# Diagonal blocks of the masked key products: strided row sums on VectorE in place of small products on TensorE

## The chip, the cores and the metric

The kernel runs on one core of one Trainium2 chip. The metric is device time in microseconds (us): the median of several executions. Engines are called TensorE or PE (matrix products; PEld is its weight load), VectorE or DVE, ScalarE or ACT, GpSimd or POOL, and SyncE or SP, which here issues transfers (DMA). Each engine takes its own instructions in order and waits on counters (semaphores) that other engines raise.

## The reference

One encoder layer over two sequences of 512 tokens, 1024 wide: an input projection whose columns feed 8 neighbourhood attention heads and 4 gated DeltaNet heads, an output projection, a layer norm, and a gated MLP with a depthwise convolution. The change is in the DeltaNet heads, the chunked delta rule. Cut to what matters (two of these run, one per direction):

```python
def _gated_delta_chunked(q, k, v, beta, g):
    ...
    gc = jnp.cumsum(g, axis=-1)
    ...
    decay = jnp.exp(jnp.where(tril, gc[..., :, None] - gc[..., None, :], -jnp.inf))
    kb = k * beta[..., None]
    lower = jnp.where(strict, jnp.einsum('bhnid,bhnjd->bhnij', kb, k) * decay, 0.0)
    a = lower + jnp.eye(c, dtype=jnp.float32)
    rhs = jnp.concatenate([v * beta[..., None], kb * jnp.exp(gc)[..., None]], axis=-1)
    sol = lax.linalg.triangular_solve(a, rhs, left_side=True, lower=True, unit_diagonal=True)
    ...
```

`lower` is the masked, decayed matrix of key products. The kernel solves with it by inverting its 16 x 16 diagonal blocks and joining the inverses level by level.

## The kernel before, in words

All arithmetic is in float32; the big projections are done as three products of split operands (`w_hi`, `w_lo`, `x_hi`, `x_lo`), with weights split by POOL. Stages follow each other: neighbourhood attention (to about 240 us), four delta heads (`delta_head(h, ...)`, h = 0 to 3, about 97 us each, to about 630 us), output projection and norm, the MLP. The order on each engine is written out by hand in one function per engine; each engine has its own `delta_head`.

In a delta head a sequence s (0 or 1) has 4 chunks (CH) of 128 tokens, and both directions g share the key products. On VectorE, in this order: `log_decays` (L1655, once the decay rows have landed), key scales, the convolution of Q for s = 0 (`convolve`, L1589, four instructions for one sequence), `lower` (L1667, from the key products in PSUM into `m_t`), then for each s the **join** of both directions' parts (L1739, into `m_t`) and the **mask** (L1741), which keeps in `u_t` only the 16 x 16 blocks on the diagonal of each 128 x 128 chunk. Then the convolutions of Q for s = 1 and of V for s = 0, two MEMSETs, and `eliminate` (L1684 to L1699), which inverts 128 blocks at once, one per partition, and raises `inv_ready`. Then the convolution of V for s = 1, `scores` (L1674), `between` (L1719), `both_directions` (L1712 to L1715) on the inverses that have come back, `expand` (L1704), `decayed_q` (L1678), and the level loop with its subtractions (L1784, L1785) and selections (L1723, L1727).

Between mask and elimination the blocks have to get from "row of the chunk per partition" to "block per partition". PE multiplies each chunk of `u_t` with `fold` (a column of 16 x 16 identities): a product of 128 x 128 by 128 x 16, whose row m holds the 16 entries of column m in its diagonal block. These products (L816) go into PSUM bank 6, after the wait for `masked` and for the copies of K out of that bank (`k_tok_ready`). ACT copies the bank into `packed` (L1307) and raises `fold_copied`. SP's `exchange` waits for that, stores `packed` to `block_dram` (L476), waits for the store, and loads the blocks twice: into half of the partitions of `packed` (L480) and into the other half of `blk` (L482). Since the two directions need a block and its transpose, `eliminate` begins with a turning copy of one half (L1684, partitions 64 to 127). After the elimination SP stores the inverses and loads them back (L485, L492).

On PE the head runs: projection of Q for s = 1 and V for s = 0 (`project`, L614), the products L816, projection of V for s = 1, projections of the gate z (two, with the key-query products L832 between them), V's transposes (L842; those for s = 1 wait for `fold_copied`, since they use bank 6), a first piece of the next head's K projection (`fill`, L639), and the level loop: L868 for both s, a fill of 5, L882 and L885 for both s, a fill of 5. At level 0 L868 waits for `c_ready` and `r_selected`, which VectorE raises in `between` and `expand`. Products of small tiles in float32 stand in the trace as two records each.

After the loop over chunks and the last products (L938, L939) the next head follows; after the fourth, the output projection (L951).

Of the kernel before, what the change touches and what calls it, by code (L numbers as in the profile page):

```python
# [8 lines left out]
AX = mybir.AxisListType  # L9

P = 128
# [21 lines left out]
CH = L // P  # L34
# [51 lines left out]
def encoder_layer(nc, xT, x_tok, ln_row, w_gate, w_all, rpb, gdn_conv, gate_vec, a_log,  # L86
# [3 lines left out]
    with ctx:  # L90
# [187 lines left out]
        def sem(name):  # L278
            names.append(name)
            return ctx.enter_context(nc.semaphore(name))  # L280
# [23 lines left out]
        ktr_done, k_tok_ready, vtr_done, vg_tok_ready, kk_done, kq_done = (  # L304
            sem("ktr_done"), sem("k_tok_ready"), sem("vtr_done"), sem("vg_tok_ready"), sem("kk_done"),
            sem("kq_done"))
        o_copied, masked, folded, fold_copied, blocks_stored, blocks_landed, eliminated = (
            sem("o_copied"), sem("masked"), sem("folded"), sem("fold_copied"), sem("blocks_stored"),
            sem("blocks_landed"), sem("eliminated"))
        inv_ready, inv_stored, d_landed, u_landed = (  # L310
            sem("inv_ready"), sem("inv_stored"), sem("d_landed"), sem("u_landed"))
# [100 lines left out]
        def _(sp):  # L412
# [59 lines left out]
            def exchange(h, last_head):  # L472

                sp.wait_ge(fold_copied, h + 1)
                sp.dma_start(block_dram.rearrange("(i b) (r c) -> (b r) i c", b=P // IB, c=IB), packed[:, 0:INST // 2, :]  # L476
                             ).then_inc(blocks_stored, 16)
                sp.wait_ge(blocks_stored, 16 * h + 16)
                half = P // 2
                sp.dma_start(packed[half:P, INST:2 * INST, :].rearrange("p i c -> p (i c)"), block_dram  # L480
                             ).then_inc(blocks_landed, 16)
                sp.dma_start(blk[0:half, :], block_dram).then_inc(blocks_landed, 16)  # L482

                sp.wait_ge(inv_ready, h + 1)
                sp.dma_start(inverse_dram.rearrange("m k n -> k m n"), inv[:, :, :]).then_inc(inv_stored, 16)  # L485
                sp.wait_ge(inv_stored, 16 * h + 16)

                for m, landed in enumerate((d_landed, u_landed)):
                    for d in range(2):
                        i0 = d * (INST // 2)  # L490
                        rows = inverse_dram[m ^ d, :, :].rearrange("(i b) (r c) -> (b r) i c", b=P // IB, c=IB)
                        sp.dma_start(packed[:, m * INST + i0:m * INST + i0 + INST // 2, :],  # L492
                                     rows[:, i0:i0 + INST // 2, :]).then_inc(landed, 16)
                for n in range(6, 8):
                    load(raw(GDN0 + n), 4 * h + (GDN0 + n))
                if not last_head:

                    sp.wait_ge(osum_done, 2 * h + 2)
                    load_decays(h + 1)
                for n in range(8, 10):  # L500
                    load(raw(GDN0 + n), 4 * h + (GDN0 + n))
# [100 lines left out]
        def _(pe):  # L602
# [182 lines left out]
            def tile(ap, c):  # L785
                return ap[:, c * P:(c + 1) * P]

            def delta_head(h, last_head):
# [19 lines left out]
                pe.wait_ge(w_ready, c + 3)  # L808
                pe.wait_ge(conv_done, 6 * h + 3)
                project(0, slot(GDN0 + 2), 0)  # L810
                pe.wait_ge(k_tok_ready, 2 * h + 1)
                for s in range(SEQS):
                    pe.wait_ge(masked, 2 * h + (s + 1))
                    for cc in range(CH):
                        n = s * CH + cc
                        ins = mm(ps[6][:, n * IB:(n + 1) * IB], tile(u_t[:, s, :], cc), fold, start=True, stop=True)  # L816
                ins.then_inc(folded, 1)

                pe.wait_ge(m_ready, 4 * h + 4)
                project(v_bank(1), slot(GDN0 + 2), 1)  # L820
                pe.wait_ge(w_ready, c + 4)
# [13 lines left out]
                for s in range(SEQS):  # L835
                    pe.wait_ge(silu_done, 6 * h + (4 + s + 1))
                    if s == 0:
                        pe.wait_ge(k_tok_ready, 2 * h + 2)
                    else:
                        pe.wait_ge(fold_copied, h + 1)  # L840
                    for cc in range(CH):
                        ins = nc.tensor.transpose(tile(ps[7 - s], cc), tile(qkv[:, VX, s, :], cc), ident)  # L842
                    ins.then_inc(vtr_done, 1)
# [273 lines left out]
        def _(act_e):  # L1117
# [134 lines left out]
            def delta_head(h, last_head):  # L1252
# [48 lines left out]
                for g in range(GROUPS):  # L1301
# [1 line left out]
                centre(h, QX, 1)  # L1303
                silu(QX, 0)
                centre(h, VX, 0)
                act_e.wait_ge(folded, h + 1)
                nc.scalar.copy(packed[:, 0:INST // 2, :].rearrange("p i c -> p (i c)"), ps[6][:, 0:INST // 2 * IB]  # L1307
                               ).then_inc(fold_copied, 1)
                silu(QX, 1)
                silu(VX, 0)  # L1310
                centre(h, VX, 1)
# [179 lines left out]
        def _(dve):  # L1491
# [139 lines left out]
            def chunks(ap):  # L1631
                return ap.rearrange("p (c n) -> p c n", c=CH)
# [5 lines left out]
            def delta_head(h, last_head):  # L1638
# [41 lines left out]
                def eliminate():  # L1680

                    half = slice(P // 2, P)
                    step(nc.vector.tensor_copy(blk[half, :].rearrange("p (r c) -> p r c", c=IB),  # L1684
                                               packed[half, INST:2 * INST, :].rearrange("p c r -> p r c")))
                    lo = blk[:, :].rearrange("p (i j) -> p i j", i=IB)
# [49 lines left out]
                for s in range(SEQS):  # L1736
                    dve.wait_ge(m_ready, 4 * h + (2 * s + 2))

                    TT(m_t[:, 2 * s, :], m_t[:, 2 * s, :], m_t[:, 2 * s + 1, :], ALU.add).then_inc(joined_l, 1)  # L1739
                    dve.wait_ge(joined_l, 2 * h + (s + 1))  # L1740
                    TT(chunks(u_t[:, s, :]), chunks(m_t[:, 2 * s, :]), bcast(same_block), ALU.mult).then_inc(masked, 1)  # L1741
                convolve(h, QX, 1)
                convolve(h, VX, 0)
                step(nc.vector.memset(inv[:, 0, :], 0.0))
# [329 lines left out]
```

## Time and profile before

| what | us |
|---|---|
| median of 3 runs | 1456.69 |
| lowest and highest run | 1456.39, 1457.8 |
| the profiled execution's own time | 1456.55 |
| its span, first to last instruction | 1454.8 |
| busy in it: PE, DVE, ACT, POOL | 1395.0, 788.5, 442.1, 479.6 |
| mean granted TensorE clock (1 is 2.4 GHz) | 0.991 |

The profile describes one execution. A busy share is an average over stages with different limits; what a stage waits for is read from the chain and the waits in it. In a timeline, "0.69 DVE L1741 ..." behind 357.31 means that the instruction started at 357.31 us and took 0.69; a row with x8 merges eight neighbours. In square brackets stands the time that the engine was idle before, and who ended it. The starts of two neighbouring VectorE instructions can be closer than the duration of the first, because they overlap a little at their ends.

### The profile page before, as it was taken

The page shows a single profiled execution, that of the slowest core. Times are in us where ns is not written, and L with a number is a line of the kernel's source. Part 1 is how long each engine was busy: PE and PEld are TensorE (multiplying, and loading weights), DVE is VectorE, ACT ScalarE, POOL GpSimd, SP SyncE. Part 2 cuts the span into 40 slices and gives each one's busy share as a digit, 9 for nine tenths or more (in the row PEclk, how much of TensorE's full clock was granted, in tenths as well). Part 3 has the DMA queues.
Part 4 walks back from the last instruction along what each step waited for, and adds up shares of the span by engine and source line. Part 5 has one row for each costly group of instructions (what it writes and reads, how often), then busy time and mean ns, then how long its engine had stood idle before and what let it go on. Part 6 is the DMA issues. An engine that isn't in the chain of part 4 may idle for free.

```text
span 1454.8 us, 18723 instructions
## 1 busy us (share of the span) xinstructions
PE 1395.0 (96%) x6959; PEld 1146.2 (79%) x6959; DVE 788.5 (54%) x1346; ACT 442.1 (30%) x924; POOL 479.6 (33%) x219
## 2 busy tenths in 40 slices
PE   7999999989899898799999999999999999999998
PEld 5777777777787787788878888888888888888886
DVE  4344447968868869633744344344344354226657
ACT  4234346327245163240522222121121122122210
POOL 3322221212121022126544344343343344454460
PEclk9999999999999999899999999999999999999999
DMA  8100011201102112033221111111111115111112
GB/s 249 45 30 30 30 44 44 50 16 60 34 23 58 29 58 50 15 131 107 90 79 45 56 43 48 53 43 51 50 43 55 46 43 193 53 43 53 49 58 101
DMA packets 49511, 87.15 MB, mean 60 GB/s; under 512 B 24432, under 2 KB 27184, under 8 KB 49456
## 3 DMA queue, kind: packets, MB, share of 16 engines
q1 hardware_dynamic: 44704, 70.41, 15.0%
q10 hardware_dynamic: 4752, 15.99, 2.9%
q8 instruction: 36, 0.59, 0.2%
q14 instruction: 19, 0.16, 0.0%
HBM read 76.66 MB, written 9.73 MB: 59 GB/s over the span
## 4 chain that ended last, share of the span: by engine, by line
issue 37%; PE 32%; DVE 16%; POOL 10%; DMA 3%; ACT 1%; POOLq 1%; SPq 0%; DVEq 0%; ACTq 0%
PE banks L639 11%; POOL w_hi L524 8%; PE banks L951 6%; PE banks L1051 3%; DVE qkv L1589 2%; DMA d_n<-decay_dram 2%; PE banks L614 1%; PE banks L748 1%; DVE att L1655 1%; PE banks L773 1%; DVE m_t L1667 1%; DVE d_n L1785 1%; PE banks L761 1%; DVE inv L1696 1%; DVE outer L1693 1%
## 5 line engine op out<-in xcount | busy, mean ns | idle before, releaser
L524 POOL TENSOR_TENSOR w_hi<-w_raw,one 128x1024 fp32r<-128x1024 f32 (+1 forms) x99 | 187.4, 1893 | 900.0 <-PE banks L614 368.3
L614 PE MATMUL banks<-x_hi,w_hi 128*128 128x512 f32 (+1 forms) x912 | 358.9, 393 | 15.8 <-POOL w_lo L527 8.3
L614 PE MATMUL banks<-x_hi,w_lo 128*128 128x512 f32 (+1 forms) x912 | 355.7, 390 | 0.0
L614 PE MATMUL banks<-x_lo,w_hi 128*128 128x512 f32 (+1 forms) x912 | 355.6, 390 | 0.0
L1905 DVE SCALAR_TENSOR_TENSOR cv<-banks,fw,cv 128x511 f32<-128x511 f32 x176 | 132.0, 750 | 261.7 <-ACT cv L1425 253.9
L527 POOL TENSOR_TENSOR w_lo<-w_raw,w_hi 128x1024 fp32r<-128x1024 f32 (+1 forms) x99 | 251.4, 2540 | 7.7
L614 PEld LDWEIGHTS banks<-x_hi,w_hi 128*128 128x128 f32 (+1 forms) x912 | 170.6, 187 | 54.9 <-POOL w_lo L527 8.3
L614 PEld LDWEIGHTS banks<-x_hi,w_lo 128*128 128x128 f32 (+1 forms) x912 | 170.6, 187 | 37.3 <-issue 0.6
L614 PEld LDWEIGHTS banks<-x_lo,w_hi 128*128 128x128 f32 (+1 forms) x912 | 170.7, 187 | 36.4 <-issue 1.1
L1425 ACT ACTIVATE cv<-banks,fw_j 128x512 f32<-128x512 f32 x88 | 68.7, 780 | 337.2 <-PE banks L614 334.7
L1934 DVE TENSOR_TENSOR a_lo<-act,a_hi 128x1024 fp32r<-128x1024 f32 x39 | 65.1, 1675 | 96.5 <-ACT a_hi L1443 96.5
L1051 PE MATMUL banks<-w_hi,a_hi 128*128 128x512 f32 x288 | 112.0, 389 | 0.0
L1051 PE MATMUL banks<-w_hi,a_lo 128*128 128x512 f32 x288 | 112.0, 389 | 0.0
L1051 PE MATMUL banks<-w_lo,a_hi 128*128 128x512 f32 x288 | 112.0, 389 | 0.0
L639 PE MATMUL banks<-x_hi,w_hi 128*128 128x512 f32 x256 | 103.7, 405 | 0.0
L639 PE MATMUL banks<-x_hi,w_lo 128*128 128x512 f32 x256 | 103.2, 403 | 0.0
L639 PE MATMUL banks<-x_lo,w_hi 128*128 128x512 f32 x256 | 103.1, 403 | 0.0
L1443 ACT CAST a_hi<-act 128x1024 fp32r<-128x1024 f32 (+1 forms) x39 | 40.8, 1053 | 147.3 <-PE banks L1051 139.3
L1589 DVE SCALAR_TENSOR_TENSOR qkv<-banks,cw_all,qkv 128x510 f32<-128x510 f32 (+1 forms) x96 | 71.3, 749 | 11.5 <-ACT qkv L1187 7.8
L1915 DVE TENSOR_TENSOR act<-cv 128x512 f32 (+1 forms) x44 | 68.4, 1554 | 9.1 <-DVE cv L1905 8.9
L1562 DVE TENSOR_TENSOR s_sb<-banks,bm 128x512 f32<-128x512 f32 x32 | 22.1, 692 | 76.7 <-PE banks L748 76.7
L1051 PEld LDWEIGHTS banks<-w_hi,a_hi 128*128 128x128 f32 x288 | 54.1, 188 | 11.3
(206 smaller groups left out, 2000.1 us busy)
## 6 DMA issues: line engine op xcount, KB each, us to landing
w_raw<-w_all SPq DMA_DIRECT2D x102, 512.0 KB, 3.2
d_n<-decay_dram SPq DMA_DIRECT2D x8, 512.0 KB, 4.7
z_tok<-x_tok ACTq DMA_DIRECT2D x8, 512.0 KB, 6.0
x_dram<-z_tok ACTq DMA_DIRECT2D x8, 512.0 KB, 2.6
z<-x_dram ACTq DMA_DIRECT2D x8, 512.0 KB, 8.2
y<-z SPq DMA_DIRECT2D x7, 512.0 KB, 2.6
mix<-xT SPq DMA_DIRECT2D x12, 256.0 KB, 8.4
gb<-ln_row ACTq DMA_DIRECT2D x4, 512.0 KB, 8.3
```

The lines of the kernel that those rows point to most:

```text
L524: nc.gpsimd.tensor_tensor(w_hi[u][:, 0:n], w_raw[ru][:, 0:n], one[:, :].to_broadcast([P, n]), ALU.mult).then_inc(w_high, 1)
L527: nc.gpsimd.tensor_tensor(w_lo[u][:, 0:n], w_raw[ru][:, 0:n], w_hi[u][:, 0:n].bitcast(F32), ALU.subtract).then_inc(w_ready, 1)
L614: last = mm(ps[bank][0:cols, :], w[u][:, k * cols:(k + 1) * cols], seq(x[:, k, :], s), start=n == 0, stop=n == 3 * KT - 1)
L639: ins = mm(ps[s][:, :], w[u][:, k * P:(k + 1) * P], seq(x[:, k, :], s), start=i == 0, stop=i == 3 * KT - 1)
L951: ins = mm(ps[b][:, :], x[k][:, t * P:(t + 1) * P], w[u][:, cols], start=k == 0 and n == 0, stop=k == KT - 1 and n == 2)
L1051: ins = mm(ps[t][:, :], x[a][:, t * P:(t + 1) * P], w[u][:, cols], start=start and i == 0, stop=stop and i == 2)
L1425: A(cv[:, b, :], ps[b][:, :], ACT.Identity, scale=fw_j[:, x, 1:2], bias=fw_j[:, x, 3:4]).then_inc(up_center, 1)
L1443: nc.scalar.copy(a_hi[a][:, :], act[:, bass.ds(k, 1), :].rearrange("p a n -> p (a n)")).then_inc(a_high, 1)
L1589: ins = STT(dst[:, a:b], src[:, a + o:b + o], cw_all[:, 3 * h + x, tap:tap + 1], dst[:, a:b], ALU.mult, ALU.add)
L1905: ins = STT(cv[:, b, a:e], ps[b][:, a + o:e + o], fw[:, bass.ds(2 * j + x, 1), tap:tap + 1].rearrange("p a b -> p (a b)"), cv[:, b, a:e], ...
L1915: TT(act[:, bass.ds(j, 1), s * L:(s + 1) * L].rearrange("p a n -> p (a n)"), cv[:, s, :], cv[:, 2 + s, :], ALU.mult).then_inc(up_act, 1)
L1934: TT(a_lo[a][:, :], act[:, bass.ds(k, 1), :].rearrange("p a n -> p (a n)"), a_hi[a][:, :].bitcast(F32), ALU.subtract).then_inc(a_ready, 1)
```

## The change

The sixteen records of L816 on PE, ACT's copy and its semaphore `fold_copied` go. VectorE itself makes `packed` from the masked tile: after each mask it waits for it (`masked`) and sums `u_t` over the eight blocks of a row, by a view with the block index innermost (step 16 floats). Since a row of a chunk has values in one block only, the sum is that row of its diagonal block. The result is the transpose of what the products gave, so the two halves of the partitions change places: in SP's two loads and in the turning copy. SP waits for `folded`, now raised by VectorE twice a head. PE's wait before V's transposes for s = 1 goes as well.

```diff
@@ exchange, on SP
-                sp.wait_ge(fold_copied, h + 1)
+                sp.wait_ge(folded, 2 * h + 2)
                 sp.dma_start(block_dram.rearrange("(i b) (r c) -> (b r) i c", b=P // IB, c=IB), packed[:, 0:INST // 2, :]
                              ).then_inc(blocks_stored, 16)
                 sp.wait_ge(blocks_stored, 16 * h + 16)
                 half = P // 2
-                sp.dma_start(packed[half:P, INST:2 * INST, :].rearrange("p i c -> p (i c)"), block_dram
+                sp.dma_start(packed[0:half, INST:2 * INST, :].rearrange("p i c -> p (i c)"), block_dram
                              ).then_inc(blocks_landed, 16)
-                sp.dma_start(blk[0:half, :], block_dram).then_inc(blocks_landed, 16)
+                sp.dma_start(blk[half:P, :], block_dram).then_inc(blocks_landed, 16)
@@ delta_head, on PE
                 project(0, slot(GDN0 + 2), 0)
-                pe.wait_ge(k_tok_ready, 2 * h + 1)
-                for s in range(SEQS):
-                    pe.wait_ge(masked, 2 * h + (s + 1))
-                    for cc in range(CH):
-                        n = s * CH + cc
-                        ins = mm(ps[6][:, n * IB:(n + 1) * IB], tile(u_t[:, s, :], cc), fold, start=True, stop=True)
-                ins.then_inc(folded, 1)
-
                 pe.wait_ge(m_ready, 4 * h + 4)
                 project(v_bank(1), slot(GDN0 + 2), 1)
...
                     if s == 0:
                         pe.wait_ge(k_tok_ready, 2 * h + 2)
-                    else:
-                        pe.wait_ge(fold_copied, h + 1)
@@ delta_head, on ACT
                 centre(h, VX, 0)
-                act_e.wait_ge(folded, h + 1)
-                nc.scalar.copy(packed[:, 0:INST // 2, :].rearrange("p i c -> p (i c)"), ps[6][:, 0:INST // 2 * IB]
-                               ).then_inc(fold_copied, 1)
                 silu(QX, 1)
@@ eliminate, on DVE
-                    half = slice(P // 2, P)
+                    half = slice(0, P // 2)
@@ delta_head, on DVE
                     TT(chunks(u_t[:, s, :]), chunks(m_t[:, 2 * s, :]), bcast(same_block), ALU.mult).then_inc(masked, 1)
+                    dve.wait_ge(masked, 2 * h + (s + 1))
+                    nc.vector.tensor_reduce(packed[:, s * CH:(s + 1) * CH, :],
+                                            u_t[:, s, :].rearrange("p (i b c) -> p i c b", i=CH, c=IB), AX.X, ALU.add
+                                            ).then_inc(folded, 1)
                 convolve(h, QX, 1)
```

The order of VectorE's instructions from the end of `lower` to the blocks of the elimination, in the kernel before:

```order
L1739 TENSOR_TENSOR m_t<-m_t 128x512 [waits m_ready]
L1741 TENSOR_TENSOR u_t<-m_t,cst 128x512 [waits joined_l]
L1739 TENSOR_TENSOR m_t<-m_t 128x512 [waits m_ready]
L1741 TENSOR_TENSOR u_t<-m_t,cst 128x512 [waits joined_l]
L1589 SCALAR_TENSOR_TENSOR qkv<-banks,cw_all,qkv 128x510 [waits center]
```

And in the changed kernel, whose lines are numbered 13 lower here (join L1726, mask L1728, convolution L1576):

```order
L1726 TENSOR_TENSOR m_t<-m_t 128x512 [waits m_ready]
L1728 TENSOR_TENSOR u_t<-m_t,cst 128x512 [waits joined_l]
L1730 TENSOR_REDUCE packed<-u_t 128x64 [waits masked]
L1726 TENSOR_TENSOR m_t<-m_t 128x512 [waits m_ready]
L1728 TENSOR_TENSOR u_t<-m_t,cst 128x512 [waits joined_l]
L1730 TENSOR_REDUCE packed<-u_t 128x64 [waits masked]
L1576 SCALAR_TENSOR_TENSOR qkv<-banks,cw_all,qkv 128x510 [waits center]
```

Each mask is followed by a TENSOR_REDUCE, and the second join, the second mask and the convolutions stand behind them; nothing else on this engine has moved. On PE, at the end of V's projection for s = 0 and the start of that for s = 1, before:

```order
L614 MATMUL banks<-x_hi,w_lo_69 128x512
L816 MATMUL banks<-cst,u_t 128x16 [waits masked,k_tok_ready]
L816 MATMUL banks<-cst,u_t 128x16 x3
L816 MATMUL banks<-cst,u_t 128x16 [waits masked]
L816 MATMUL banks<-cst,u_t 128x16 x3
L614 MATMUL banks<-x_hi,w_hi_68 128x512 [waits m_ready]
```

And in the changed kernel:

```order
L614 MATMUL banks<-x_hi,w_hi_68 128x512
L614 MATMUL banks<-x_lo,w_hi_68 128x512
L614 MATMUL banks<-x_hi,w_lo_69 128x512
L614 MATMUL banks<-x_hi,w_hi_68 128x512 [waits m_ready]
L614 MATMUL banks<-x_lo,w_hi_68 128x512
```

The two projections now stand next to each other, with the wait for `m_ready` alone between them.

## Rows read from the trace of the kernel before

**Rows 1.** The page: busy time of PE, and the chain by engine.

```profile
PE 1395.0 (96%) x6959; PEld 1146.2 (79%) x6959; DVE 788.5 (54%) x1346; ACT 442.1 (30%) x924; POOL 479.6 (33%) x219
...
issue 37%; PE 32%; DVE 16%; POOL 10%; DMA 3%; ACT 1%; POOLq 1%; SPq 0%; DVEq 0%; ACTq 0%
```

**Rows 2.** The chain, 356 to 392 us: by line; a piece (start, us, what).

```profile
by line: DVE qkv L1589 24.7%; DVE inv L1696 9.1%; DVE outer L1693 9.1%; DVE d_n L1704 7.0%; DVE u_t L1719 6.9%; DVE q_d L1678 6.7%; DVE att L1674 6.6%; issue 6.4%; DVE u_t L1741 3.8%; DVE m_t L1739 3.8%; DVE m_t L1704 3.3%; DVE m_t L1667 2.
...
391.70 0.60 DVE d_n L1784
```

**Rows 3.** Waits, 248 to 630 us: us in total, times, longest.

```profile
PE banks L868 <- issue: 11.8, 4, 3.7
...
DVE blk L1684 <- DMA blk<-block_dram: 0.6, 1, 0.6
```

**Rows 4.** VectorE's groups by shape, 200 to 640 us: busy us, mean ns | idle before.

```profile
L1565 DVE TENSOR_REDUCE nmax<-s_sb 128x2 f32<-128x512 f32 x9 | 6.2, 686 | 0.3
...
L1713 DVE TENSOR_TENSOR packed<-packed,cst 128x128 f32<-128x128 f32 x8 | 2.3, 292 | 0.3
...
L1684 DVE COPY blk<-packed 64x256 f32<-64x256 f32 x4 | 1.5, 385 | 0.7 <-DMA blk<-block_dram 0.6
```

**Rows 5.** Timeline of VectorE in head 2.

```profile
356.44 0.84 DVE L1739 TENSOR_TENSOR m_t<-m_t 128x512 f32<-128x512 f32 x1
357.31 0.69 DVE L1741 TENSOR_TENSOR u_t<-m_t,cst 128x512 f32<-128x512 f32 x1
357.92 0.68 DVE L1739 TENSOR_TENSOR m_t<-m_t 128x512 f32<-128x512 f32 x1
```

**Rows 6.** Timeline of PE in head 2, around the products.

```profile
357.62 0.39 PE L614 MATMUL banks<-x_lo,w_hi 128*128 128x512 f32 x1
357.85 0.39 PE L614 MATMUL banks<-x_hi,w_lo 128*128 128x512 f32 x1
...
359.38 1.06 PE L816 MATMUL banks<-cst,u_t 128*128 128x16 f32 x8 [0.20 <-DVE u_t L1741]
360.30 0.47 PE L614 MATMUL banks<-x_hi,w_hi 128*128 128x512 f32 x1
```

**Rows 7.** Timeline of ACT in head 2: the copy.

```profile
360.49 0.27 ACT L1307 COPY packed<-banks 128x128 f32<-128x128 f32 x1 [1.53 <-PE banks L816]
```

**Rows 8.** SP's queue: the store and the load behind it, heads 2 and 3.

```profile
360.78 0.38 SPq L476 DMA_DIRECT2D block_dram<-packed  x1
362.94 0.46 SPq L480 DMA_DIRECT2D packed<-block_dram  x1
...
457.96 0.38 SPq L476 DMA_DIRECT2D block_dram<-packed  x1
460.82 0.45 SPq L480 DMA_DIRECT2D packed<-block_dram  x1
```

**Rows 9.** The chain behind head 4, 570 to 680 us.

```profile
628.82 51.35 PE banks L951 x220
```

**Rows 10.** A stretch of head 1: us, busy of each engine, PEclk, DMA share, GB/s.

```profile
298.00:302.00 4.00, 3.19 (x12) 2.98 (x13) 2.47 (x5) 0.75 (x2) 0.00 (x0) 0.57 0.02 4
```

**Rows 11.** Timeline of PE: L868 at level 0 in heads 1 and 2.

```profile
286.49 2.02 PE L868 MATMUL banks<-x,u_t 128*128 128x128 f32 x16 [2.36 <-issue]
...
383.72 3.65 PE L868 MATMUL banks<-x,u_t 128*128 128x128 f32 x16 [2.70 <-issue]
```

**Rows 12.** Pieces of the chain at level 1 in heads 1, 2 and 3.

```profile
298.81 2.05 PE banks L868 x8
300.86 1.66 PE banks L639 x5
...
396.04 1.13 PE banks L868 x8
397.17 1.17 PE banks L639 x5
...
493.46 2.05 PE banks L868 x8
```

More of the change, by code:

```diff
@@ L306, in encoder_layer @@
             sem("kq_done"))
-        o_copied, masked, folded, fold_copied, blocks_stored, blocks_landed, eliminated = (
-            sem("o_copied"), sem("masked"), sem("folded"), sem("fold_copied"), sem("blocks_stored"),
+        o_copied, masked, folded, blocks_stored, blocks_landed, eliminated = (
+            sem("o_copied"), sem("masked"), sem("folded"), sem("blocks_stored"),
             sem("blocks_landed"), sem("eliminated"))
```

## The prediction

> **What bounds the kernel now.** I first read busy time and the chain over the whole span. The page has PE busy for 96% of it [rows 1], which looks like a kernel where anything taken off TensorE is time won. The chain says something else: PE holds 32% of it and DVE 16% [rows 1]. So there are stages in which PE is busy and still not what the end waits for. The change touches only the four delta heads (the passes of `delta_head` for h = 0 to 3, called heads 1 to 4 here). I then read the chain in order of time for the part of head 2 that holds the change, 356 to 392 us. Its summary by line names only VectorE lines and 6.4% of issue; there is no PE piece among those it names [rows 2]. From the joins of the key products to the first subtraction of level 0 (L1784, 391.70) the chain stays on VectorE: join, mask, two convolutions, elimination, convolution, scores, expansions.
>
> The third view is who waits for whom. PE waits four times, 11.8 us in all and up to 3.7, in front of L868, the first product of level 0 ("issue" names no releaser; by the code it is `r_selected`, which the expand of L1704 signals) [rows 3]. Once in each head PE reaches the level loop 2 to 4 us before VectorE, and PE is in order. This is the slack that decides the case: work taken off PE ahead of it lengthens a wait, and work put on VectorE ahead of it moves everything behind.
>
> **Added: two row sums a head on VectorE.** In the order of the changed kernel each mask (L1741) is followed by a TENSOR_REDUCE that waits for it, and only then come the next join and the convolutions. Duration: the TENSOR_REDUCE that this trace has (L1565, 512 elements in) takes 686 ns [rows 4]. The new one differs in two ways: it writes 64 sums instead of 2, and its innermost step is 16 floats (64 bytes). The nearest row with that step is the turning copy into `blk` (L1684): 385 ns for 256 elements [rows 4]. If all of that scaled, 512 elements would take 0.77 us; that is my upper bound. For the lower bound, 128 elements take 292 ns (L1713) [rows 4], so 384 more elements cost 686 - 292 = 394 ns, 1.03 ns each; that copy plus 256 elements at this pace is 0.65. I choose 0.69, the row of the same operation with the same element count.
>
> The Trainium skill speaks against this instruction: "SBUF — State Buffer", section "Door 1: The DMA port swizzle", says that an access which crosses into another 16-byte line costs extra, and every read of the new sum does. It gives no price; the rival below has it. The copy at L1684 steps just as far and shows no doubling, so I give the rule little weight.
>
> What one adds to the engine is more than its duration, since it depends on the mask. The rows of head 2 [rows 5]: the independent second join starts at 357.92, 0.61 us after the mask started at 357.31 (so 0.08 before the mask's end); an operation that waits for its predecessor starts about 0.03 us after its end (join 356.44 plus 0.84 is 357.28, mask at 357.31). So mask to sum is 0.69 + 0.03 = 0.72 in place of 0.61 (+0.11), and sum to the next, independent instruction 0.69 - 0.08 = 0.61. One sum costs 0.72 us, two 1.44 a head, 5.76 in four heads. With 0.65 and 0.77 it is 5.4 and 6.4.
>
> **Removed: the products and the copy.** The eight products a head stand in the trace as sixteen records (L816). In head 2 they stand between the projection's products at 357.85 and 360.30 [rows 6]; at the projection's spacing (357.62 to 357.85, 0.23) the second would start at 358.08. PE is rid of 360.30 - 358.08 = 2.2 us a head, 8.9 in all. It lies in front of the wait at L868, with three projections of 24 matmuls between, none of which VectorE's chain needs earlier: the convolution of V's second half stands behind the elimination anyway. I cost the gain at nothing. Its cover is PE's wait; with it gone the gain would be the first rival's. The copy (0.27 us) was in ACT's queue at 360.49 to 360.76 [rows 7]; ACT then waits for convolutions, so it too is worth nothing.
>
> **Moved: when the blocks leave.** SP's store waited for that copy and went at 360.78 [rows 8]. In the new order: sum of s = 0 at 358.03, join 358.64, mask 359.36, second sum 360.08 to 360.77. The store goes at the same instant. But VectorE reaches the blocks (L1684) 1.44 us later than now, so the round trip is better covered. In head 3 it was late: store at 457.96, loads only at 460.82, against 360.78 and 362.94 in head 2 [rows 8], and VectorE waited 0.63 us, the only such wait (0.6, once) [rows 3]. It goes: -0.63. What is late next there is VectorE itself. The swapped halves (partitions 0 to 63 and 64 to 127) change places of two loads of equal size; nothing. `inv_ready` and with it POOL's split, the inverses' round trip and V's transposes all start from VectorE and shift with it. Of the waits dropped on PE, the one for `masked` held 0.20 us in head 2 [rows 6], which is inside the 2.2, and none is seen for `fold_copied`.
>
> **Sum.** 5.76 - 0.63 = +5.1 us. Nothing behind takes it back: after level 0 VectorE and PE wait for each other in turn, the next head's decays are loaded after this head's last products, and after head 4 the chain goes straight on to the output products (L951, 51.35 us without a break) [rows 9]. The profiled execution has 1456.55 us (span 1454.8), so 1461.7; the median of the runs is 0.14 above it, so **1461.8 us**, +0.35%.
>
> **The rivals.** *PE's stream decides (faster).* If PE came to L868 later than `r_selected`, its 2.2 us a head would count and VectorE's 1.44 be hidden: 1456.7 - 8.9 = 1447.8. For it: 96% busy. Against: the four waits of rows 3. It decides only where PE's wait there is zero; in heads 1 and 2 it is 2.36 and 2.70 us [rows 11]. 3%.
>
> *The clock gives some back (within 0.2%).* PE will be idle 2.2 + 1.44 = 3.7 us longer in each head before L868, part of it already at the transposes of V. Now the clock is at its upper level, 2.4 GHz, except in stretches like 298 to 302, whose granted clock of 0.57 has most of the time at 1.2 GHz [rows 10]. Where the low stretch lies decides its price. In head 2 it fell behind the wait for level 0: sixteen records of L868 took 3.65 us after 2.70 us of idle [rows 11], hidden under VectorE's expansions. In head 1 it fell in level 1, on the chain: L868 and the fill 2.05 + 1.66 against 1.13 + 1.17 in head 2, 1.4 us dearer [rows 12]; head 3's L868 takes 2.05 too. With a longer wait at level 0 heads 1 and 3 may behave like head 2: -2.8, 1459.0 us. Against it: V's transposes and the first fill break the idle time in two, and no row shows an idle time like the new one. 17%. *The clock costs more*: a low stretch falls on level 1 of head 2 as well, or a second one in some head: +1.4 to +2.8, 1463.2 to 1464.6. 12%.
>
> **How the numbers follow.** Forecast 62%, PE decides 3%, clock gives back 17%, clock costs more 12%, slow sum 6%. Around the forecast alone it is 1461.4 to 1462.4 from the sum's bounds and about 1 us each way from where low-clock stretches fall. For 8 in 10 the range takes in both clock cases and leaves out the slow sum and PE: **1458.3 to 1464.9**. A measurement of this kernel can tell about 0.2% (2.9 us) from no change, so the border is at 1459.6: slower 62 + 12 + 6 = 80%, less a little for a forecast that comes out small, 0.79; same 0.18; faster 0.03.
>
> **What would show it.** Right: eight TENSOR_REDUCE of 0.65 to 0.77 us; no wait before `blk`; waits before L868 grown from 11.8 us by about 8 to 14 in all heads (counting those at V's transposes); from a head's first join to its first subtraction of level 0 about 1.4 us more. Wrong: sums over 1 us; a subtraction of level 0 that waits for L885; PE's wait at L868 shorter than now; or a span of the level loops that differs between heads by more than the sums, with the granted clock telling it.

## The result

| kernel | median us (lowest to highest) | against the kernel before |
|---|---|---|
| before, 6 runs | 1456.74 (1456.39 to 1457.8) | |
| changed, 6 runs | 1462.93 (1460.54 to 1465.33) | 1.0043, interval 1.003 to 1.0055 |

The changed kernel is slower by 6.2 us; 1461.8 was forecast, in a range of 1458.3 to 1464.9. Two more comparisons (e5 and e10 below) gave 1.0044 (1.0028 to 1.006) and 1.0041 (1.0028 to 1.0054). The profiled execution of the changed kernel took 1465.25 us, near the top of its runs.

### The profile after

The page, busy time and the chain by engine (to be read against [rows 1]):

```profile
PE 1394.0 (95%) x6895; PEld 1142.5 (78%) x6895; DVE 797.5 (54%) x1354; ACT 439.7 (30%) x920; POOL 479.8 (33%) x219
...
issue 37%; PE 32%; DVE 17%; POOL 10%; DMA 2%; ACT 1%; POOLq 1%; SPq 0%; DVEq 0%; ACTq 0%
```

PE has 64 instructions fewer and the span is longer. VectorE is busy 9.0 us more (797.5 - 788.5) for eight instructions more, so one of them costs more than the 0.69 us that I had taken. The timeline of VectorE in head 2, as in [rows 5] (join L1726, mask L1728, the new sum L1730, convolution L1576, turning copy L1671):

```profile
358.57 0.68 DVE L1726 TENSOR_TENSOR m_t<-m_t 128x512 f32<-128x512 f32 x1
359.29 0.69 DVE L1728 TENSOR_TENSOR u_t<-m_t,cst 128x512 f32<-128x512 f32 x1
360.02 1.04 DVE L1730 TENSOR_REDUCE packed<-u_t 128x64 f32<-128x512 f32 x1
360.98 0.68 DVE L1726 TENSOR_TENSOR m_t<-m_t 128x512 f32<-128x512 f32 x1
361.69 0.69 DVE L1728 TENSOR_TENSOR u_t<-m_t,cst 128x512 f32<-128x512 f32 x1
362.42 1.03 DVE L1730 TENSOR_REDUCE packed<-u_t 128x64 f32<-128x512 f32 x1
363.38 6.10 DVE L1576 SCALAR_TENSOR_TENSOR qkv<-banks,cw_all,qkv 128x510 f32<-128x510 f32 x8
...
369.94 0.37 DVE L1671 COPY blk<-packed 64x256 f32<-64x256 f32 x1
```

The joints are as forecast: 0.04 us from the mask's end to the sum, 0.08 us of overlap behind it. The duration is not: 1.04 us. From the first mask to the convolutions it is now 4.09 us (359.29 to 363.38), against 1.94 in the kernel before (357.31 to 359.25), whose second mask and first convolution stand so:

```profile
358.64 0.69 DVE L1741 TENSOR_TENSOR u_t<-m_t,cst 128x512 f32<-128x512 f32 x1
359.25 0.74 DVE L1589 SCALAR_TENSOR_TENSOR qkv<-banks,cw_all,qkv 128x510 f32<-128x510 f32 x1
```

By shape, the new sums beside the old ones of the attention stage (busy us, mean ns):

```profile
L1730 DVE TENSOR_REDUCE packed<-u_t 128x64 f32<-128x512 f32 x8 | 8.3, 1037 | 0.3
L1552 DVE TENSOR_REDUCE nmax<-s_sb 128x2 f32<-128x512 f32 x9 | 6.2, 686 | 0.3
```

Who waited for whom, 248 to 640 us, answering [rows 3]:

```profile
PE banks L832 <- ACT qkv L1245: 11.8, 4, 3.0
...
PE banks L858 <- issue: 11.0, 4, 4.9
```

No wait before the turning copy is left. PE's wait at level 0 (now L858) is 11.0 us, and it waits a further 11.8 before V's second transposes (L832). Together 22.8 against 11.8: at these two places PE idles 11 us more.

### Where the time went, by stretches

From the starts in VectorE's timeline I made the table below: in each head from the first join to the turning copy, from there to the first subtraction of level 0, and from there to the last subtraction of the level loops; then from the last of these in head 4 to the end of the span. The stretch between one head's level loops and the next head's first join is not in it. Four numbers are heads 1 to 4; "before 2" and "changed 2, 3" are further profiles of the same kernels (e12, e5, e10).

| profile | join to blocks | blocks to level 0 | level loops | rest |
|---|---|---|---|---|
| before | 9.23, 9.38, 9.82, 9.23 | 25.43, 25.80, 25.44, 25.45 | 19.55, 18.13, 19.51, 18.11 | 850.6 |
| before 2 | 9.22, 9.29, 10.13, 9.24 | 25.42, 25.78, 25.42, 25.43 | 18.12, 18.12, 18.14, 17.44 | 853.3 |
| changed | 11.36, 11.37, 11.35, 11.37 | 25.39, 25.42, 25.40, 25.41 | 19.58, 19.51, 18.13, 17.43 | 853.4 |
| changed 2 | 11.36, 11.36, 11.39, 11.37 | 25.43, 25.44, 25.44, 25.42 | 18.13, 19.46, 18.12, 17.44 | 853.3 |
| changed 3 | 11.36, 11.37, 11.38, 11.37 | 25.41, 25.42, 25.43, 25.43 | 18.14, 19.58, 18.13, 17.43 | 853.5 |
| e1, products off | 9.22, 9.32, 9.21, 9.22 | 26.03, 25.77, 25.42, 25.45 | 18.11, 18.13, 18.14, 17.39 | 853.3 |
| e2, sums added | 11.32, 11.32, 11.32, 11.31 | 25.43, 25.42, 25.44, 25.43 | 19.48, 19.46, 18.12, 17.42 | 853.4 |
| e9, the same again | 11.32, 11.47, 11.30, 11.31 | 25.42, 25.43, 25.44, 25.44 | 19.71, 19.71, 18.13, 17.91 | 853.5 |

The first column is the change. In the changed kernel its sum repeats to 0.03 us: 45.45 to 45.48, against 37.66 and 37.88 in the two profiles of the kernel before, so 7.6 to 7.8 us more. The second gives 0.3 to 0.5 back. So does a stretch that the table leaves out: in front of head 3 VectorE waits 1.4 to 1.7 us for the decay rows in the changed kernel, where it waited 2.3 and 2.6, and the way from head 2's last subtraction to head 3's first join is 43.0 to 43.3 us in place of 43.7 and 44.0.

The third column is the clock. A level loop takes 18.1 or about 19.5 us in heads 1 to 3, depending on whether a stretch at 1.2 GHz falls on the chain. The records of PE's first product of a level (L868, in the changed kernel L858) show where it falls, here in heads 1 and 2 of "changed 3":

```profile
288.40 3.76 PE L858 MATMUL banks<-x,u_t 128*128 128x128 f32 x16 [1.85 <-issue]
...
300.72 1.13 PE L858 MATMUL banks<-x,u_t 128*128 128x128 f32 x8 [1.27 <-DVE x L1710]
...
386.16 2.02 PE L858 MATMUL banks<-x,u_t 128*128 128x128 f32 x16 [2.06 <-issue]
...
398.48 2.04 PE L858 MATMUL banks<-x,u_t 128*128 128x128 f32 x8 [1.27 <-DVE x L1710]
```

In heads 1 to 3 of all eight profiles it is one or the other. Either the sixteen records of level 0 are slow (2.5 to 3.8 us), which VectorE's work hides, and the eight of level 1 take 1.13; or those of level 0 take 2.02, and the eight of level 1 take 1.7 to 2.05 on the path. The kernel before had the second form in heads 1 and 3 of one profile and in no head of the other, so the form alone does not tell the two kernels apart.

The last column differs by 2.7 us for the same reason. Between 630 and 1445 us every profile but my first of the kernel before has one stretch of a lower granted clock, between 730 and 760. In that first profile the clock stays at 1.00 there, in the second it drops:

```profile
736.00:743.00 7.00, 6.17 (x20) 4.92 (x21) 2.27 (x4) 0.98 (x2) 0.07 (x1) 0.76 0.30 112
```

(us, PE, PEld, DVE, ACT, POOL busy, granted clock, DMA share, GB/s.) So the difference of the two spans, 8.7 us, holds 2.8 us that the change did not make; the medians are the better measure.

### The profile page after: what moved, and what is told of

The parts are those of the page before. It is cut to its first block, busy times and chain, and to the rows that moved or that the text cites. A ratio compares the mean times of both kernels' runs of the same rounds, so it can differ in the third digit from the quotient of the medians.

```text
span 1463.5 us, 18591 instructions
## 1 busy us (share of the span) xinstructions
PE 1394.0 (95%) x6895; PEld 1142.5 (78%) x6895; DVE 797.5 (54%) x1354; ACT 439.7 (30%) x920; POOL 479.8 (33%) x219
## 4 chain that ended last, share of the span: by engine, by line
issue 37%; PE 32%; DVE 17%; POOL 10%; DMA 2%; ACT 1%; POOLq 1%; SPq 0%; DVEq 0%; ACTq 0%
PE banks L639 11%; POOL w_hi L524 8%; PE banks L941 6%; DVE qkv L1576 3%; PE banks L1041 3%; DMA d_n<-decay_dram 2%; PE banks L614 2%; PE banks L748 1%; DVE att L1642 1%; PE banks L773 1%; DVE m_t L1654 1%; DVE d_n L1776 1%; PE banks L761 1%; DVE inv L1683 1%; DVE outer L1680 1%
## 5 line engine op out<-in xcount | busy, mean ns | idle before, releaser
L1576 DVE SCALAR_TENSOR_TENSOR qkv<-banks,cw_all,qkv 128x510 f32<-128x510 f32 (+1 forms) x96 | 71.2, 748 | 11.3 <-ACT qkv L1177 7.8
L1041 PEld LDWEIGHTS banks<-w_lo,a_hi 128*128 128x128 f32 x288 | 54.1, 188 | 11.3
```

The source lines that it names most:

```text
L1041: ins = mm(ps[t][:, :], x[a][:, t * P:(t + 1) * P], w[u][:, cols], start=start and i == 0, stop=stop and i == 2)
L1576: ins = STT(dst[:, a:b], src[:, a + o:b + o], cw_all[:, 3 * h + x, tap:tap + 1], dst[:, a:b], ALU.mult, ALU.add)
```

## The experiments

In all comparisons the kernel before ran on the same chip: medians 1456.0 us beside e1 to e4, 1455.1 beside e5 to e8, 1456.2 beside e9 to e12.

### e1 and e2: one half of the change at a time

e1 takes the products off, in the kernel before:

```diff
-                pe.wait_ge(k_tok_ready, 2 * h + 1)
-                for s in range(SEQS):
-                    pe.wait_ge(masked, 2 * h + (s + 1))
-                    ...
-                ins.then_inc(folded, 1)
...
-                act_e.wait_ge(folded, h + 1)
-                nc.scalar.copy(packed[...], ps[6][...]).then_inc(fold_copied, 1)
+                act_e.wait_ge(masked, 2 * h + 2)
+                A(packed[...], ps[6][...], ACT.Copy, scale=0.0).then_inc(fold_copied, 1)
```

> The kernel before with the sixteen L816 records taken off TensorE and nothing put on VectorE; the copy stays on ScalarE and writes zeros, so the diagonal blocks are missing from the result. Theory (VectorE holds the path, TensorE only waits longer before level 0): 1456.7 us, within 1.5 us. Rival 1 (freed TensorE time is worth something): down to 1447.8. Rival 2 (longer idle time before level 0 costs clock on the path by itself): 1458 to 1462, with more stretches of a low granted clock in level 1 than before.

Measured: 1454.67 us, 0.9988 (0.9978 to 0.9997), 1.3 us faster by the medians. By its interval the products are worth something, though far from 8.9 us, and not all of it need be TensorE's time. ACT's copy no longer waits for the products, so the blocks leave earlier: in head 3 the store goes 3.1 us after the first join (4.2 in the kernel before), and the wait of 0.6 to 0.9 us for the blocks is gone. Its level loops are all short, like those of "before 2".

e2 leaves the products in and adds the sums beside them:

```diff
                     TT(chunks(u_t[:, s, :]), ..., bcast(same_block), ALU.mult).then_inc(masked, 1)
+                    dve.wait_ge(masked, 2 * h + (s + 1))
+                    nc.vector.tensor_reduce(inv[:, 1, s * CH * IB:(s + 1) * CH * IB].rearrange("p (i c) -> p i c", c=IB),
+                                            u_t[:, s, :].rearrange("p (i b c) -> p i c b", i=CH, c=IB), AX.X, ALU.add
+                                            ).then_inc(extra_sum, 1)
```

> The kernel before, complete, with the two row sums a head added on VectorE beside the products (their result goes to a scratch place and is not used). Theory: four times 2.14 us (a sum takes 1.04 us in the changed kernel, its wait for the mask costs 0.11, and one wait for the blocks of 0.6 us is covered): 1464.0 us, or 1462.9 like the changed kernel if the low-clock stretches give the same back. Rival (taking the products off is worth something in the changed kernel): slower than the changed kernel by 2 us or more, 1465 and above.

Measured: 1465.62 us, 1.0073 (1.0059 to 1.0087), +9.6. Join to blocks is 11.32 us in each head: VectorE alone gives the whole first column of the table. The time is above both numbers of the theory and speaks for the rival, but the changed kernel had been timed on another chip.

### e9 and e10: the same question on one chip

e9 is e2 again, e10 the changed kernel again, side by side.

> The kernel before, complete, with the two unused row sums a head added on VectorE, now beside the changed kernel on the same chip. Theory 1 (taking the products off is worth nothing while TensorE waits before level 0): the same time as the changed kernel, within 1.5 us. Theory 2 (it is worth something even so, as the 1465.6 of the first time against 1462.9 on another chip hinted): 2 us or more slower than the changed kernel.

> The changed kernel a third time, as the other side of the comparison above: 5 to 8 us over the kernel before; join to blocks 11.36 us, level loops of 17.4 to 19.5 us in some pattern.

Measured: e9 1466.12 us, 1.0068 (1.0055 to 1.0081); e10 1462.65 us, 1.0041 (1.0028 to 1.0054). The difference of 3.5 us is outside what I had allowed, and e2 says the same. **The theory that the freed TensorE time is worth nothing falls**: beside the sums, taking off the products, with the copy and the waits that hang on them, is worth about 3.5 us. Where these 3.5 us lie is not shown. In e9 PE waits for the second mask behind the sum of s = 0:

```profile
263.39 1.79 PE L817 MATMUL banks<-cst,u_t 128*128 128x16 f32 x8 [1.24 <-DVE u_t L1742]
...
PE banks L817 <- DVE u_t L1742: 5.0, 4, 1.2
```

This wait was 0.7 us in four heads in the kernel before. In e9 there follow stretches at half clock under V's projection in heads 1 and 2, where the kernel before had 1.00 over the same windows:

```profile
263.50:270.50 7.00, 7.00 (x21) 5.84 (x22) 6.79 (x10) 0.96 (x3) 0.00 (x0) 0.51 0.16 28
362.50:369.50 7.00, 6.99 (x21) 5.89 (x22) 6.79 (x9) 0.90 (x2) 0.00 (x0) 0.51 0.14 28
```

They are not the cause as they stand. PE's wait at level 0 hides them (6.8 us in all are left of it, 14.6 in e2), and e2, the same kernel, has 1.00 in both windows. What is longer on the path is the level loops, 74.5 us in sum in e2 and 75.5 in e9, against 73.2 to 74.7 in three profiles of the changed kernel; but the two profiles of the kernel before are 3.5 us apart in this column (75.3 and 71.8), so two profiles can't tie it to the kernel. The two profiled executions of the kernel with sums added took 1464.9 and 1465.8 us; its slowest runs (1468.5, 1469.6) have no trace. The 3.5 us are measured, their cause stays open.

### e3, e4 and e8: what makes the sum long

e3 changes only how the sum reads, `"p (i c b) -> p i c b"` in place of `"p (i b c) -> p i c b"`.

> The changed kernel, whose row sum reads eight neighbouring floats for each of its 64 sums in place of eight floats 64 bytes apart, so the blocks and the result are wrong. Theory 1 (the step of 64 bytes makes the sum 1.04 us long): 0.69 us each, and 8 times 0.35 us less: 1460.1 us. Theory 2 (the number of sums written, 64 in place of 2, makes it long): 1.04 us as before, 1462.9.

Measured: eight sums of 686 ns (5.5 us busy in place of 8.3), join to blocks 10.66 us, 1460.59 us, 1.0031 (1.0011 to 1.005). The step makes it long, the 64 results don't, and this kernel has the sums that I had forecast: +4.6 us where my sum said +5.1.

e4 gives each of the eight places a form of its own:

```diff
+                    step_of = {(0, 0): 16, (0, 1): 1, (1, 0): 2, (1, 1): 4, (2, 0): 8}.get((h, s))
...
+                        src = u_t[:, s, :].rearrange("p (x n k) -> p x k n", n=8, k=step_of)
```

> The changed kernel with another form of the row sum in each of its eight places, all over 512 floats (the result is wrong): 64 sums of 8 floats with a step of 16, 1, 2, 4 and 8 floats, 16 sums of 32 floats with a step of 16, 2 sums of 256 neighbours, 16 sums of 32 neighbours. Theory 1 (step): 0.69 us for steps 1 to 4 and for the neighbours, more for 8 and 16, 1.04 for both forms with a step of 16. Theory 2 (number of sums): 1.04 us for all five with 64 sums, about 0.77 for 16 sums, 0.69 for 2, whatever the step. Between them: each adds a part.

The timeline, in the order of the list above (one execution, 1463.44 us):

```profile
261.31 1.04 DVE L1741 TENSOR_REDUCE packed<-u_t 128x64 f32<-128x512 f32 x1
263.71 0.69 DVE L1741 TENSOR_REDUCE packed<-u_t 128x64 f32<-128x512 f32 x1
358.78 0.69 DVE L1741 TENSOR_REDUCE packed<-u_t 128x64 f32<-128x512 f32 x1
360.83 1.06 DVE L1741 TENSOR_REDUCE packed<-u_t 128x64 f32<-128x512 f32 x1
457.83 1.12 DVE L1741 TENSOR_REDUCE packed<-u_t 128x64 f32<-128x512 f32 x1
460.31 1.02 DVE L1741 TENSOR_REDUCE packed<-u_t 128x16 f32<-128x512 f32 x1
555.65 0.69 DVE L1741 TENSOR_REDUCE packed<-u_t 128x2 f32<-128x512 f32 x1
557.70 0.69 DVE L1741 TENSOR_REDUCE packed<-u_t 128x16 f32<-128x512 f32 x1
```

Steps of 1 and 2 floats cost 0.69 us; steps of 4, 8 and 16 cost 1.06, 1.12 and 1.04. The border lies between 8 and 16 bytes, and beyond it the cost is about the same. Theory 1 is right in kind and wrong in one place (a step of 4 floats is slow already). This agrees with the Trainium skill, "SBUF — State Buffer", section "Door 1: The DMA port swizzle", in that it wants at least two accesses in each 16-byte line: two floats of step 2 share one, two of step 4 don't. The same passage calls a stride of 4 fp32 free, and there the measurement decides: 1.06 us against 0.69.

e8 asks why the turning copy had not shown this. Its extra operations stand at the very start of the kernel:

```diff
+            step(nc.vector.tensor_copy(w[2], w[0]))
+            step(nc.vector.tensor_copy(flat_[2], turn[0]))
+            step(nc.vector.tensor_copy(turn[2], flat_[0]))
+            step(TT(w[2], w[0], w[1], ALU.add))
+            step(TT(flat_[2], turn[0], flat_[1], ALU.add))
+            step(TT(turn[2], flat_[0], flat_[1], ALU.add))
+            step(TT(flat_[2], turn[0], turn[1], ALU.add))
+            step(nc.vector.tensor_copy(w[2][0:64, 0:256], w[0][0:64, 0:256]))
```

> The changed kernel with eight extra VectorE operations on scratch at its very start, each waiting for the one before (they cost some 6 us there and change no result): over 128 x 512 floats a copy from neighbours to neighbours, reading with a step of 16, writing with a step of 8; an addition of neighbours, with one operand read with a step of 16, writing with a step of 8, with both operands read with a step of 16; and a copy of 64 x 256 neighbours. Theory 1 (reading a float every 64 bytes has a pace of its own, about 1.7 ns, in every operation): 1.04 us for all that read so, 0.69 for the rest. Theory 2 (the copy with a step shows 385 ns for 256 because only sums are slow): 0.69 us for copies and additions alike.

(The two operations that write with a step write with 16 floats, not 8 as the expectation says.) In the order of the diff (one execution, 1468.92 us with the extra operations):

```profile
3.32 0.43 DVE L1494 COPY bm<-bm 128x512 f32<-128x512 f32 x1
3.78 0.59 DVE L1495 COPY bm<-bm 128x512 f32<-128x512 f32 x1
4.41 0.63 DVE L1496 COPY bm<-bm 128x512 f32<-128x512 f32 x1
5.07 0.69 DVE L1497 TENSOR_TENSOR bm<-bm 128x512 f32<-128x512 f32 x1
5.79 1.02 DVE L1498 TENSOR_TENSOR bm<-bm 128x512 f32<-128x512 f32 x1
6.84 1.72 DVE L1499 TENSOR_TENSOR bm<-bm 128x512 f32<-128x512 f32 x1
8.60 1.86 DVE L1500 TENSOR_TENSOR bm<-bm 128x512 f32<-128x512 f32 x1
10.49 0.29 DVE L1501 COPY bm<-bm 64x256 f32<-64x256 f32 x1
```

Neither theory holds as written. A copy of neighbours has a faster pace than an addition or a sum (0.43 against 0.69 us for 512), and the step costs it 0.16 us; it lands at 0.59, still below an addition of neighbours. An addition with one stepped operand takes 1.02, as long as the stepped sum. So the copy of [rows 4], 385 ns for 256 where neighbours take 0.29 us, had been slowed by its step all along. I read its 385 ns as the price of a stepped read that is not dear.

### e6: turning the data in the mask

The mask writes the blocks turned, so that the sum reads neighbours.

```diff
-                    TT(chunks(u_t[:, s, :]), chunks(m_t[:, 2 * s, :]), bcast(same_block), ALU.mult).then_inc(masked, 1)
+                    TT(u_t[:, s, :].rearrange("p (i c b) -> p i b c", i=CH, c=IB),
+                       m_t[:, 2 * s, :].rearrange("p (i b c) -> p i b c", i=CH, c=IB),
+                       same_block.rearrange("p (b c) -> p b c", c=IB).unsqueeze(1).to_broadcast([P, CH, P // IB, IB]),
+                       ALU.mult).then_inc(masked, 1)
```

> The changed kernel, whose mask writes its blocks turned (with a step of 8 floats, 32 bytes), so that the row sum reads eight neighbouring floats; the result is the right one. Theory 1 (only a read with a step of 16 bytes and more is slow): mask 0.69 us, sum 0.69 us, so 2.8 us less than the changed kernel of the same chip. Theory 2 (a write with such a step is as slow as a read): mask 1.04 us, sum 0.69 us, and the same time as the changed kernel.

```profile
L1728 DVE TENSOR_TENSOR u_t<-m_t,cst 128x512 f32<-128x512 f32 x8 | 9.2, 1150 | 0.3
L1733 DVE TENSOR_REDUCE packed<-u_t 128x64 f32<-128x512 f32 x8 | 5.5, 686 | 0.3
```

The sum is back at 686 ns and the mask has grown from 692 to 1150: a stepped write costs more than the stepped read it replaces. 1463.32 us, 1.0049 (1.0032 to 1.0065), beside 1462.83 of the changed kernel (e5). Theory 2.

### e5 and e12: how much one profile tells

> The changed kernel as it is, beside the kernels below on one chip. Theory (VectorE: 2.14 us more a head between a head's first join and the blocks, 7.8 us in all; up to 1.4 us a head back or more where the low-clock stretches fall): 5 to 8 us over the kernel before, eight sums of 1.04 us. In the profile the stretch from join to blocks 11.36 us in every head as in the first profile; the level loops 18.1 or 19.5 us, in another pattern over the heads than in the first. Rival (the pattern of the level loops belongs to the kernel): 19.6, 19.5, 18.1, 17.4 us again.

> The kernel before as it is, for a second profile of it. Theory (where low-clock stretches fall differs from run to run): level loops of 18.1 or 19.5 us in another pattern than 19.6, 18.1, 19.5, 18.1 us; join to blocks 9.2 to 9.4 us except where a store is late; and from the last subtraction of head 4 to the end 853.4 us as in the six kernels since. Rival (the pattern belongs to the kernel): the same pattern, and 850.6 us to the end.

e5: 1462.83 us, 1.0044 (1.0028 to 1.006). e12, one execution: 1455.6. Both are in the table of stretches. Join to blocks and blocks to level 0 repeat, except for one late store in head 3 of the kernel before; the level loops and the rest do not belong to the kernel. These are the first pieces of the chain at level 1 of head 1, in the changed kernel and in e12, to be read against [rows 12]:

```profile
300.63 2.05 PE banks L858 x8
302.67 1.70 PE banks L639 x5
```

```profile
298.28 1.13 PE banks L868 x8
299.41 1.16 PE banks L639 x5
```

In the first profiles of both kernels a low stretch lay there (and 2.05 + 1.66 in [rows 12]); in e12, e5, e10 and e1 it does not.

### e7 and e11: work taken off VectorE

If VectorE's queue holds the path, the two masks should go from it, not come with two sums. In e7 GpSimd makes them (it has little to do there), the products stay, and cover for the blocks' round trip is moved ahead of the elimination.

```diff
@@ on POOL, at the start of split_for_next
+                for s in range(SEQS):
+                    pool.wait_ge(joined_l, 2 * h + (s + 1))
+                    nc.gpsimd.tensor_tensor(u_t[:, s, :].rearrange("p (c n) -> p c n", c=CH),
+                                            m_t[:, 2 * s, :].rearrange("p (c n) -> p c n", c=CH),
+                                            same_block.unsqueeze(1).to_broadcast([P, CH, P]), ALU.mult).then_inc(masked, 1)
@@ delta_head, on DVE
-                    dve.wait_ge(joined_l, 2 * h + (s + 1))
-                    TT(chunks(u_t[:, s, :]), chunks(m_t[:, 2 * s, :]), bcast(same_block), ALU.mult).then_inc(masked, 1)
                 convolve(h, QX, 1)
                 convolve(h, VX, 0)
+                for s in range(SEQS):
+                    between(0, s)
+                dve.wait_ge(silu_done, 6 * h + 3)
+                for g in range(2):
+                    decayed_q(g)
```

(`between(0, s)` and the first two `decayed_q` are taken out of their old places.)

> The kernel before (products and copy as they were), with the two masks of a head on GpSimd in place of VectorE, and with the two products of `between` for level 0 and two of the four `decayed_q` moved ahead of the elimination, to stand over the blocks' round trip; the result is the right one. Theory (VectorE's queue holds the path, so work taken off it counts): 4 times 1.33 us less on VectorE, 5.3 us, less what slows it beside GpSimd (0.16 us a join where they meet in the kernel before): 1451 to 1454 against 1456.5. Rival (the round trip of the blocks becomes the limit, since the mask on GpSimd takes 1.2 us in place of 0.69 and the store leaves later): VectorE waits before the turning copy for as long as it gained, 1456 to 1458.

GpSimd's masks by shape (busy us, mean ns):

```profile
L558 POOL TENSOR_TENSOR u_t<-m_t,cst 128x512 f32<-128x512 f32 x8 | 11.6, 1464 | 4.2 <-DVE m_t L1744 4.2
```

Measured: **1451.41 us, 0.997 (0.9959 to 0.9982)**, 3.7 us faster than the kernel before by the medians; it is the fastest of the study. From the join to the first subtraction of level 0 its heads take 33.70, 33.28, 33.90 and 33.20 us, against 34.64, 35.07, 35.55 and 34.67 in "before 2": 5.9 us less, where 5.3 was expected. Of the two profiles, its level loops are the longer ones (73.2 us in sum against 71.8), so that its span is 4.5 below that of e12. VectorE in head 2: both joins, then the convolutions with nothing between, then the moved pieces over the round trip:

```profile
354.13 1.35 DVE L1744 TENSOR_TENSOR m_t<-m_t 128x512 f32<-128x512 f32 x2
355.40 6.10 DVE L1594 SCALAR_TENSOR_TENSOR qkv<-banks,cw_all,qkv 128x510 f32<-128x510 f32 x8
361.42 1.28 DVE L1724 TENSOR_TENSOR u_t<-m_t,cst 128x512 f32<-128x512 f32 x2
362.62 1.29 DVE L1683 TENSOR_TENSOR q_d<-qkv,d_n 128x512 f32<-128x512 f32 x2
363.91 0.27 DVE L1752 MEMSET inv<- 128x256 f32 x1
364.26 0.07 DVE L1753 MEMSET inv<- 128x16 f32 x1
364.37 0.38 DVE L1689 COPY blk<-packed 64x256 f32<-64x256 f32 x1
```

e11 moves only the masks.

> The kernel before with the two masks of a head on GpSimd and nothing else moved; the result is the right one. Theory (the blocks' round trip becomes the limit): a mask takes 1.46 us there, the products end about 1.3 us later than now and VectorE comes 1.33 us earlier, so it waits 2 to 2.5 us before the turning copy in each head, and the time is that of the kernel before or up to 4 us more: 1455 to 1460. Rival (the masks off VectorE are all of the gain of the kernel with moved pieces): 1451 to 1452 as there.

Measured: 1462.64 us, 1.005 (1.0035 to 1.0066), slower than expected by 2.6 us. The wait that was foreseen is there, 10.2 us in four:

```profile
367.82 0.38 DVE L1689 COPY blk<-packed 64x256 f32<-64x256 f32 x1 [2.32 <-DMA blk<-block_dram]
...
DVE blk L1689 <- DMA blk<-block_dram: 10.2, 4, 3.2
```

Join to blocks is 41.1 us in sum, 3.3 more than in "before 2". So a shorter queue on VectorE is lost to the round trip where nothing covers it; the gain of e7 needs its cover. Its profiled execution is 1461.5 us, and its span 5.9 above that of e12, of which 3.3 lie between join and blocks, 1.0 between blocks and level 0, and 1.5 in the level loops. The moved pieces without the move of the masks were not run; since the kernel before waits for the blocks only once, 0.6 to 0.9 us, I would expect no more than that from them.

## Why the prediction was right, and where not

- **What bounds the heads: right.** The stretch from join to blocks grew by 2.1 us, what VectorE got, in heads 1 and 4 (2.0 in head 2; 1.5 in head 3, where a wait was covered), in every profile, with the products (e2) and without them.
- **The cost of a sum: wrong, too small by half.** The step that failed is the upper bound of 0.77 us: a copy's 385 ns, doubled, stood for a sum's stepped read, and the value 0.69 rested on a row of neighbours. Measured: 1.04 us. With it the term is 0.11 + 1.04 - 0.08 = 1.07, 2.14 a head, 8.6 in all, not 5.76. The rival that doubled it (1467.3) was too dear; the truth lies half way. The rule on 16-byte lines (the Trainium skill, "SBUF — State Buffer"), to which I gave little weight, was right in kind; it has no price. Sums over 1 us were among my own signs of being wrong. e3, with the step taken out, measured +4.6 against the +5.1 of the sum.
- **The blocks' round trip: right.** The 0.6 us wait went, none came; in e12 the kernel before has it again, at 0.9 us.
- **The freed TensorE time at nothing: wrong, though far nearer than the first rival's 8.9 us.** Taking the products off is worth 1.3 us by the medians in the kernel before (e1), of which 0.6 to 0.9 can be the wait for the blocks, and about 3.5 us beside the sums (e10 against e9). PE does wait longer before level 0, 22.8 us as forecast (11.8 plus 8 to 14), so its own time is covered; by which way the products still cost something beside the sums stays open.
- **The clock rivals: not decided by this change.** Heads whose low stretch falls on level 0 instead of level 1 exist, as "gives some back" had it, but the kernel before has them too: level loops of 75.3 and 71.8 us in sum there, 73.2 to 74.7 in the changed kernel.
- **"Nothing behind takes it back": not quite.** The stretch from blocks to level 0 and the wait for the decay rows of head 3 give back about 1.1 us together.
- **The total** of 1461.8 against 1462.93 came out partly by luck: the sums were put 2.8 us too low (8.56 - 5.76), and some 1.7 us came back that I had put at zero, of which the line above has about 1. The range had room for both.
- **The reading that one profile's level loops belong to the kernel: wrong.** I built the price of 2.8 us for heads 1 and 3 on it. "Before 2" has no low stretch on the chain in heads 1 to 3.

## What to carry to other kernels

Read an instruction's price off a row of the same operation with the same access pattern; a row of another operation, even one that steps just as far, can hide the step behind a pace of its own. Turning the data costs wherever it is done, here less in the read than in the write. When a queue is the path, ask which of its pieces another engine can take, and give the transfer behind them cover before they leave.

## What the runs showed of the hardware

- VectorE, float32, 128 x 512: a sum that reads at a step of 16, 32 or 64 bytes takes 1.02 to 1.12 us against 0.69 at 4 and 8 bytes (e4), an addition with one operand read at 64 bytes 1.02, with both 1.86 (e8). Writing with a step of 32 bytes makes a multiplication 1.15 (e6), with one of 64 bytes an addition 1.72 (e8). A copy: 0.43, reading at 64 bytes 0.59, writing at 64 bytes 0.63 (e8).
- GpSimd takes 1.46 us for a 128 x 512 multiplication of float32 where VectorE takes 0.69 (e7).
- On an unchanged kernel the places of the stretches at 1.2 GHz moved from one profile to the next, and with them single stretches of the program by 1.4 to 2.7 us (before and e12).
